# Attention probabilities turned through VectorE and DRAM instead of TensorE, in a two-block transformer kernel

## The reference

```
q = partial_rope(q)                    # 16 heads of 64
k = partial_rope(k)                    # 2 key heads, each shared by 8 query heads
s = q . k * 64**-0.5                   # chunks of 64 queries see their own and the two chunks before
m = max(max(s), sink)
p = exp(s - m)
o = (p / (sum(p) + exp(sink - m))) @ v # the probabilities are what is turned
a = (o * silu(za)) @ w_att_out
```

## Time and profile before

| | |
|---|---|
| median of three runs | 1270.37 us (1270.3 to 1270.75) |
| profiled execution | 1270.71 us, of it span 1268.9 |
| granted TensorE clock | 0.999 of full speed |
| TensorE busy | 1261.5 us, 99% |
| VectorE busy | 893.3 us, 70% |
| ScalarE busy | 619.7 us, 49% |
| GpSimd busy | 724.1 us, 57% |

### The profile page before, as it was taken

One profiled execution on the slowest core, in us unless ns is written; L12 is line 12 of the kernel. 1 busy time (PEld: TensorE's weight loads), 2 busy tenths in 40 slices (PEclk: granted clock), 3 DMA queues, 4 the chain that ended last, 5 costly groups with the idle time before them and its releaser, 6 DMA issues.

```text
span 1268.9 us, 19753 instructions
## 1 busy us (share of the span) xinstructions
PE 1261.5 (99%) x7542; PEld 1091.2 (86%) x7542; DVE 893.3 (70%) x1380; ACT 619.7 (49%) x989; POOL 724.1 (57%) x513
## 2 busy tenths in 40 slices
PE   9999999999999999999999999999999999999998
PEld 7877877777888899989988998877778899999886
DVE  6775555777444599558855869766656999998587
ACT  6123533565334555325522546354556656666454
POOL 3543433434543588658865866444333786666767
PEclk9999999999999999999999999999999999999999
DMA  7253176564423335353535335333522233225351
GB/s 225 87 150 108 42 199 159 144 187 125 124 75 100 100 100 166 100 166 100 167 101 166 103 106 174 108 88 88 137 67 68 76 121 100 89 83 199 100 210 73
DMA packets 205371, 154.89 MB, mean 122 GB/s; under 512 B 67488, under 2 KB 194976, under 8 KB 204512
## 3 DMA queue, kind: packets, MB, share of 16 engines
q1 hardware_dynamic: 204800, 153.06, 40.3%
q10 hardware_dynamic: 480, 0.59, 0.1%
HBM read 136.20 MB, written 14.16 MB: 118 GB/s over the span
## 4 chain that ended last, share of the span: by engine, by line
PE 96%; ACT 1%; DVE 1%; DMA 1%; POOL 1%; issue 0%; SPq 0%; ACTq 0%
PE gemm L961 16%; PE gemm L962 16%; PE gemm L969 16%; PE gemm L1235 10%; PE gemm L1234 10%; PE gemm L1239 10%; PE gemm L985 2%; PE gemm L986 2%; PE gemm L991 2%; PE gemm L1018 2%; PE gemm L1019 2%; PE gemm L1024 2%; PE mix L1355 1%; PE mix L1343 1%; PE mix L1332 1%; DMA raw<-w_in 1%
## 5 line engine op out<-in xcount | busy, mean ns | idle before, releaser
L793 POOL TENSOR_TENSOR wlo<-raw,whi 128x512 fp32r<-128x512 f32 x264 | 368.7, 1428 | 288.6 <-ACT whi L1491 269.1
L961 PE MATMUL gemm<-hh,whi 128*128 128x512 f32 x544 | 215.3, 396 | 0.2 <-ACT whi L1491 0.2
L962 PE MATMUL gemm<-hl,whi 128*128 128x512 f32 x544 | 212.4, 390 | 0.0
L813 POOL TENSOR_TENSOR wlo<-raw,whi 128x512 fp32r<-128x512 f32 x108 | 159.4, 1501 | 40.5 <-ACT whi L1685 32.4
L1491 ACT ACTIVATE whi<-raw 128x2048 fp32r<-128x2048 f32 x62 | 118.4, 1909 | 46.0 <-PE gemm L969 19.8
L969 PE MATMUL gemm<-hh,wlo 128*128 128x512 f32 x544 | 136.0, 391 | 0.0
L1234 PE MATMUL gemm<-hh,whi 128*128 128x256 f32 x496 | 124.8, 284 | 0.0
L961 PEld LDWEIGHTS gemm<-hh,whi 128*128 128x128 f32 x544 | 102.1, 188 | 26.3 <-issue 4.3
L1235 PE MATMUL gemm<-hl,whi 128*128 128x256 f32 x496 | 124.4, 284 | 0.0
L962 PEld LDWEIGHTS gemm<-hl,whi 128*128 128x128 f32 x544 | 102.3, 188 | 20.4
L969 PEld LDWEIGHTS gemm<-hh,wlo 128*128 128x128 f32 x544 | 101.7, 188 | 20.9
(11 more groups left out here) (545 smaller groups left out, 3124.6 us busy)
## 6 DMA issues: line engine op xcount, KB each, us to landing
raw<-w_in SPq DMA_DIRECT2D x53, 1024.0 KB, 5.3
raw<-w_gu SPq DMA_DIRECT2D x44, 512.0 KB, 5.2
raw<-w_down SPq DMA_DIRECT2D x16, 512.0 KB, 4.4
p_rows<-p_blocks SPq DMA_DIRECT2D x32, 160.0 KB, 3.2
p_t<-p_rows SPq DMA_DIRECT2D x8, 640.0 KB, 4.0
raw<-w_o SPq DMA_DIRECT2D x5, 1024.0 KB, 5.2
raw_b<-w_branch SPq DMA_DIRECT2D x16, 256.0 KB, 6.8
blk_b<-w_o SPq DMA_DIRECT2D x8, 512.0 KB, 7.1
```

Source lines behind the costliest of these rows:

```text
L793: last = nc.gpsimd.tensor_tensor(a(wlo), a(raw), as_f32(a(whi)), ALU.subtract)
L813: return nc.gpsimd.tensor_tensor(part_of(wlo, u, b), raw_block(u, f, k), as_f32(part_of(whi, u, b)), sub)
L961: mm(bank[:, :], w, xh[:, k, :], start=(k == 0), stop=False)
L962: mm(bank[:, :], w, xl[:, k, :], start=False, stop=False)
```

## The change

For the first 12 of the 16 v, the probabilities are no longer turned by TensorE. VectorE transposes them in blocks of 32x32 (`w_blockwise`) and sorts the blocks as it writes, into one of two buffers of 128x1024. SyncE stores the buffer with four DMAs of 128 KB (one for each 32 partitions) to `w_rows` in DRAM, in runs of 256 elements, waits until they have landed, and loads it back with one DMA of 512 KB into `w_turned_p`. TensorE multiplies with the values straight from there, reading four runs of 32 elements for each block of 128 queries, in slot 2v + 5. The last four v are handled as before. ScalarE's exponentials wait for the block transposes instead of TensorE's turns.

On SyncE's queue the stores and loads are placed by hand among the weight loads. The loads of the layer norm's scale, shift and the gate's bias (`lng`, `lnb`, `bsb`), whose memory the new buffers use, move from the end of the first block to behind the last values that read the buffers. In `turned_through` the wait for the output of two heads before is now ahead of the stores.

```diff
@@ constants, buffers
+        w_blocks = [place(f"w_blocks{i}", [P, 1024], Z0 + at) for i, at in enumerate((80, 98))]
+        w_turned_p = [place(f"w_turned_p{i}", [P, 1024], Z0 + 68 + 4 * i) for i in range(2)]
+        BY_DMA = 12
+        S_PE = 2 * BY_DMA
+        w_rows = nc.dram_tensor("w_rows", (2, P, 1024), f32, kind="Internal").ap()
@@ turned_through
                 sp.wait_ge(sem("p_turned"), i + 1)
-                for f in range(4):
...
                 if 2 <= i < HEADS + 2:
                     sp.wait_ge(sem("mo_o"), i - 1)
                 elif i >= HEADS + 2:
                     sp.wait_ge(sem("st_o"), i - HEADS - 1)
+                for f in range(4):
...
@@ SyncE
+            def store_probs(v):
+                sp.wait_ge(sem("w_tb"), v + 1)
+                if v >= 2:
+                    sp.wait_ge(sem("w_v"), 2 * v - 2)
+                for f in range(4):
+                    sp.dma_start(w_rows[v % 2].rearrange("(j a) c -> a j c", a=32)[:, :, 256 * f:256 * f + 256],
+                                 w_blocks[v % 2][32 * f:32 * f + 32, :].rearrange("a (j c) -> a j c", j=4)).then_inc(sem("w_stored"), 16)
+            def load_probs(v):
+                sp.wait_ge(sem("w_stored"), 64 * (v + 1))
+                sp.dma_start(w_turned_p[v % 2][:, :], w_rows[v % 2]).then_inc(sem("w_in"), 16)
...
+            load_wide(0)
+            store_probs(5)
+            load_probs(5)
+            store_probs(6)
+            load_probs(6)
             swap_rotary(3)
             store_turned(4)
+            load_wide(1)
+            store_probs(7)
+            store_turned(5)
+            load_probs(7)
+            load_wide(2)
+            store_probs(8)
+            store_turned(6)
+            load_probs(8)
+            load_wide(3)
+            store_turned(7)
+            for v in (9, 10):
+                store_probs(v)
+                load_probs(v)
+            slot_free(n_ao)
+            load(n_ao, cols(w_ao, 0, UC))
+            store_probs(11)
+            load_probs(11)
+            sp.wait_ge(sem("w_v"), S_PE)
+            sp.dma_start(lng[:, :], ln_g.partition_broadcast(P)).then_inc(sem("c2_in"), 16)
...
@@ TensorE, w_values
-                pe.wait_ge(sem("w_pt"), s + 1)
+                if s < S_PE:
+                    pe.wait_ge(sem("w_in"), 16 * (s // 2 + 1))
+                    by_block = w_turned_p[s // 2 % 2].rearrange("p (f k b) -> p k f b", k=8, b=32)
+                    turned = lambda k: by_block[:, s % 2 * 4 + k]
+                else:
+                    pe.wait_ge(sem("w_pt"), s - S_PE + 1)
+                    turned = lambda k: wpt[:, s % 2, k * P:(k + 1) * P]
@@ TensorE, w_slot
-                    for s in (i - 4, i - 3):
-                        if 0 <= s < STEPS:
-                            w_values(s)
-                if 0 <= i - 2 < STEPS:
+                first = i - 4 if i % 2 == 0 else i - 5
+                if (S_PE <= first < STEPS) if i % 2 == 0 else (0 <= first < S_PE):
+                    w_values(first)
+                    w_values(first + 1)
+                if S_PE <= i - 2 < STEPS:
                     w_turn(i - 2)
@@ ScalarE, w_exp
-                    if s >= 3:
-                        act.wait_ge(sem("w_t"), s - 2)
+                    if s >= S_PE + 3:
+                        act.wait_ge(sem("w_t"), s - 2 - S_PE)
+                    elif s >= 3:
+                        act.wait_ge(sem("w_tb"), (s - 3) // 2 + 1)
@@ VectorE
+            def w_blockwise(v_):
+                dve.wait_ge(sem("w_p"), 2 * v_ + 2)
+                if v_ >= 2:
+                    dve.wait_ge(sem("w_stored"), 64 * (v_ - 1))
+                blocks = w_blocks[v_ % 2].rearrange("p (j k b) -> p k j b", j=4, b=32)
+                for s in (2 * v_, 2 * v_ + 1):
+                    probs = wp[:, s % 3].rearrange("p h (k j b) -> p (h k) j b", j=4, b=32)
+                    own = blocks[:, s % 2 * 4:s % 2 * 4 + 4]
+                    if s % TT == 0:
+                        for k in (1, 3):
+                            last = v.transpose(own[:, k], probs[:, k])
+                    else:
+                        last = v.transpose(own, probs)
+                last.then_inc(sem("w_tb"), 1)
@@ VectorE, w_slot, behind w_norm(i // 2)
+                    if i < S_PE:
+                        w_blockwise(i // 2)
@@ VectorE, layer_norm_first
+                dve.wait_ge(sem("c2_in"), 64)
```

More of the change, by code:

```diff
@@ L630, in turned_through @@
                 sp.wait_ge(sem("p_turned"), i + 1)
-                for f in range(4):
-                    sp.dma_start(p_rows[i % 2].rearrange("(j a) (k c) -> a k j c", a=32, c=P)[:, :, :, 32 * f:32 * f + 32],
-                                 p_blocks[32 * f:32 * f + 32, :].rearrange("a (k j b) -> a k j b", j=4, b=32)).then_inc(sem("p_stored"), 16)
                 if 2 <= i < HEADS + 2:
@@ L637, in turned_through @@
                     sp.wait_ge(sem("st_o"), i - HEADS - 1)
+                for f in range(4):
+                    sp.dma_start(p_rows[i % 2].rearrange("(j a) (k c) -> a k j c", a=32, c=P)[:, :, :, 32 * f:32 * f + 32],
+                                 p_blocks[32 * f:32 * f + 32, :].rearrange("a (k j b) -> a k j b", j=4, b=32)).then_inc(sem("p_stored"), 16)
                 sp.wait_ge(sem("p_stored"), 64 * (i + 1))
@@ L719, in store_turned @@
                                  x_turned[m % 4][32 * f:32 * f + 32, :].rearrange("a (j b) -> a j b", b=32)).then_inc(sem("x_stored"), 16)
[L721 to L734, removed]
@@ L735, in _ @@
-            slot_free(n_vs)
+            def store_probs(v):
[8 more added lines that the diff above has]
+                sp.dma_start(w_turned_p[v % 2][:, :], w_rows[v % 2]).then_inc(sem("w_in"), 16)
@@ L736, in load_wide, with load_qz @@
+            def load_qz(n):
+                slot_free(n)
+                p, j = divmod(n - n_qz, 2)
+                load(n, cols(w_in2, (I2_ZA if j else I2_Q) + p * UC, UC))
             def load_wide(u):
+                slot_free(n_vs + u)
                 slot = raw[:, (n_vs + u) % 2].rearrange("p (k a) c -> p k (a c)", a=2)
                 load(n_vs + u, cols(w_in2, I2_VS + u // 2 * 512, 512, 4 * (u % 2), 4), slot)
+            load_qz(n_qz)
+            load_qz(n_qz + 1)
+            sp.wait_ge(sem("key_s"), 1)
@@ new lines, in _ @@
+            for a, b in ((0, 8), (8, 0)):
+                for kv in range(2):
+                    sp.dma_start(key_t[a:a + 8, kv, :], key_s[64 * kv + b:64 * kv + b + 8, :]).then_inc(sem("key_in"), 16)
+            load_qz(n_qz + 2)
+            swap_rotary(0)
+            load_qz(n_qz + 3)
+            load_qz(n_qz + 4)
+            store_probs(0)
+            swap_rotary(1)
+            load_probs(0)
+            store_turned(0)
+            load_qz(n_qz + 5)
+            store_probs(1)
+            store_turned(1)
@@ L740, in _ @@
+            load_probs(1)
+            load_qz(n_qz + 6)
+            store_probs(2)
+            load_probs(2)
+            store_probs(3)
+            load_probs(3)
+            swap_rotary(2)
+            store_turned(2)
+            load_qz(n_qz + 7)
+            store_probs(4)
+            store_turned(3)
+            load_probs(4)
             load_wide(0)
+            store_probs(5)
+            load_probs(5)
+            store_probs(6)
+            load_probs(6)
             swap_rotary(3)
@@ L743, in _ @@
+            sp.wait_ge(sem("w_v"), S_PE)
+            sp.dma_start(lng[:, :], ln_g.partition_broadcast(P)).then_inc(sem("c2_in"), 16)
+            sp.dma_start(lnb[:, :], ln_b.partition_broadcast(P)).then_inc(sem("c2_in"), 16)
+            sp.dma_start(bsb[:, :, :].rearrange("p g i -> p (g i)"), sg_b.partition_broadcast(P)).then_inc(sem("c2_in"), 16)
             for u in range(1, 4):
[L744 to L747, removed]
+                slot_free(n_ao + u)
+                load(n_ao + u, cols(w_ao, u * UC, UC))
@@ L1338, in w_turn @@
                 pe.wait_ge(sem("w_p"), s + 1)
-                if s >= 1:
-                    pe.wait_ge(sem("w_pt"), s)
+                if s > S_PE:
+                    pe.wait_ge(sem("w_pt"), s - S_PE)
                 for h in range(2):
@@ L1355, in w_values @@
                         last = mm(M[3][64 * h:64 * h + 64, c * P:(c + 1) * P], v2[:, c - 1 + kb_, kv * DH:(kv + 1) * DH],
-                                  wpt[:, s % 2, (2 * h + kb_) * P:(2 * h + kb_ + 1) * P],
+                                  turned(2 * h + kb_),
                                   start=(kb_ == keys_of(c)[0]), stop=(kb_ == 1))
@@ L1846, in w_turned @@
             def w_turned(s):
-                act.wait_ge(sem("w_t"), s + 1)
-                if s >= 2:
+                act.wait_ge(sem("w_t"), s + 1 - S_PE)
+                if s >= S_PE + 2:
                     act.wait_ge(sem("w_v"), s - 1)
@@ L2636, in _ @@
             T = tiles_before(n_e0)
-            dve.wait_ge(sem("c2_in"), 64)
+            dve.wait_ge(sem("c2_in"), 16)
             tile_ready(T)
```

(2 more changed lines are left out.)

4 lines of the change are left out of this document (removed).

## The result

The changed kernel takes 1273.93 us (median of seven executions, 1271.99 to 1275.72), the kernel before 1270.37 (seven, 1270.27 to 1270.75); the ratio is 1.0026, 95% interval 1.0015 to 1.0037. It is slower by 0.26%, where I had forecast 1264.2. The profiled execution took 1273.12, its span is 1271.3 at a granted clock of 0.999. The other six executions were granted 0.995 to 0.998, so the profile shows one of the milder ones.

The account below looks back on a forecast made before the run. TensorE, busy 1261.5 of 1268.9 us, was taken as the bound. Turns removed 7.1, less VectorE's 0.4 and the trip's 0.5, made 6.2 us, giving 1264.2; its own range was 1263 to 1266, the full range 1262.0 to 1268.3.

Parts of the forecast that it names:

- What goes from TensorE: Attention stage: turns of 24 of 32 steps leave, 8.0 us, less 0.5 and 0.4 for gaps: net 7.1 us.
- The moving operand: Values on TensorE: reading four runs of 32 elements instead of contiguous ones costs nothing extra.
- Rival 4: TensorE's 84 value products: reads in runs of 128 bytes make the kernel slower, 1275.5 if doubled; chance 0.06.
- VectorE, 0.4 us: 15 us of block transposes, mostly in idle time; lag of 1 to 1.5 us per v costs TensorE 0.4 us.
- The trip, 0.5 us: Through DRAM: 8.5 us (bounds 7.2 and 10.8) against five slots, with 0.5 us of waits in slots 23 to 27.
- SyncE's queue: Trip's stores, waits and loads stand among weight loads; the next weight load queues behind each wait, only one tightly.
- The tight load: Second wide unit's weight load, issued at 895.13 and split by ScalarE at 903.07, has 2.6 us to spare.
- The sum: 7.1 - 0.4 - 0.5 = 6.2 us gained, giving a median of 1264.2.
- Rival 2: VectorE's lag and the trip take 3 us or more, 1266 to 1269; chance 0.14.
- rival 3: Weight load held behind the stores stalls ScalarE by 6 us in sum, no gain, 1268 to 1272; chance 0.04.
- the trip's length: Slower by the DRAM trip itself: gain gone at 14.6 us, 1279 at a 17 us trip; chance 0.03.
- What would show it: Signs in the trace, such as TensorE's DMA waits on w_turned_p at v = 9 to 11 only, 1 us or less.

Follow-up runs that it names:

- run 9: The changed kernel with block transposes moved to the odd slot behind the gate product and the last four x2_rows stores behind the last probabilities load: 1265.26 us, 0.9962.
- run 4: The kernel before with the changed kernel's 30 block transposes added on VectorE at the same places, into an unread scratch buffer: 1274.97 us, 1.0030.
- run 12: The kernel before with the 30 block transposes added on VectorE in the odd slot, behind the multiplication for attention's output: 1270.34 us, 0.9999.
- run 10: The changed kernel with only the block transposes moved to the odd slot behind the gate product, SyncE's queue as it was: 1270.43 us, 0.9997.
- run 7: The changed kernel with only the last four x2_rows stores moved behind the last load of probabilities on SyncE's queue: 1275.01 us, 1.0036.
- run 1: The changed kernel with block transposes cut to one 128x32 per v (wrong probabilities), all transfers and waits kept: 1270.48 us, 0.9999.
- run 3: The changed kernel with short block transposes and also values from k2's columns that don't wait for the trip: 1264.40 us, 0.9955.
- run 2: The changed kernel with the first 24 steps' values computed from k2's columns, not waiting for the trip (wrong output), transposes and DMAs kept: 1274.38 us, 1.0031.

## Why the prediction was wrong

**What goes from TensorE, 7.1 us: the mechanism right, the term 1 us too large.** The six pairs came out at 1.02 each, 6.1 us; run 9's span is 1268.9 - 1262.8 = 6.1 below that of before (its profiled execution was the fastest of five; the medians differ by 5.2). The prediction named 6.2 as its bound with all gaps in full, and nearly so they came: in run 9 the large product ahead of the values at 849.40 starts 0.32 before them, and the one behind them takes 0.34 to its follower.

**The moving operand, 0: right.** 1.15 us after, 1.15 before. Rival 4 is out.

**VectorE, 0.4 us: this step failed.** The transposes' durations were right (670 and 291 ns in the median against the 0.67 to 0.70 taken). Wrong was to take their cost as a lag of 1 to 1.5 us a v in the wide stage, felt at softmax 12. I asked how busy VectorE is and not what stands behind the new work in its order. Behind it stands `att_t`, and behind that, through ScalarE's in-order copy, the weights of the large products. On the kernel before this alone costs 4.5 us (run 4), and nothing in the other place (run 12). The path from `att_t` to `wlo` had no term in the sum; it holds the longest wait, 2.10 us.

**The trip, 0.5 us: the length right in part, the start wrong.** From the store's issue to TensorE's start it is 10.0 us after, of which the load's issue is 6.2 in; in run 10 the trip takes 924.33 - 915.53 = 8.8. I had taken 8.5, bounds 7.2 and 10.8; v = 5, behind a fresh weight load, took 11.9, over the upper bound. The loads landed in 3.7 us in the median (taken: 3.6), the stores in 3.6, where I had said 2 to 3.2. What I left out above all is that the trip can't always start when its data are ready. With VectorE in good order a trip that starts late is enough to bring the kernel back to 1270.43 (run 10).

**SyncE's queue: this step failed too.** I followed what is queued behind the trip (the weight loads), and not what the trip is queued behind, though the diff shows `store_turned` ahead of the loads and stores of probabilities. In the change it holds the load for v = 4 back until VectorE has turned other rows, and in run 10 the store of v = 9 by 4.8 us. The tight load that I named was not what stalled: it went at 895.44 and ScalarE split it at 901.76, with 0.40 us of wait for it.

**The sum.** Forecast -7.1 + 0.9 = -6.2 us. Measured, in the stage: -6.1 + 8.8 = +2.7, of it 7.8 us in waits that the trace lists. Of the remaining 1 us I estimate 0.65 as part of the same waits: a wait is listed from the end of the product before it, which lasts 0.39, where without a wait scores or values would have started 0.32 behind that product's start and a large product 0.23 (seven waits and one). The last 0.3 stays open. The waits were some nine times what I put down, and the median execution of the change, at a granted clock of 0.998, is another 0.8 us longer; a fall of the clock had no term in the sum either. Rival 2 had the mechanism in part (a lag of VectorE and a late trip), with 1266 to 1269 at most; rival 3, a stall of ScalarE ahead of a weight split, has the other part, by another way than a late load. As slower kernels I had thought only of the operand and the trip's length; the operand cost nothing, and the trip's length is at most the wait of v = 5, 0.54 us.

**What would show it.** "Waits for a DMA on w_turned_p, at v = 9 to 11 only": they came at v = 4 and 5 too (0.58 and 0.54 us at 878.17 and 888.14), and the wait for `wlo` was on no list of mine.

## What to carry to other kernels

Work put on an engine with idle time was free here only where nothing that another engine waited for stood behind it (run 12 against run 4). So write down the order of the engine around the new work, and follow each result one engine further, here VectorE to ScalarE to GpSimd to TensorE. For a transfer, list what its queue holds ahead of it, with the time to issue, as well as behind. And where two causes each make the same thing late, undoing one can show nothing (run 7) or less than half of the gain (run 10); try both together before a cause is dropped.

## What the runs showed of the hardware

**TensorE's clock after a wait.** In run 10, TensorE's timeline around the longest wait, and the windows of all engines in the same stretch (PE, PEld, DVE, ACT and POOL busy, then the granted clock, DMA share, GB/s):

```profile
924.33 1.27 PE L1419 MATMUL mix<-w_turned_p,v 128*64 128x128 f32 x16 [3.49 <-DMA w_turned_p<-w_rows]
925.54 0.80 PE L1043 MATMUL gemm<-whi,hh 128*128 128x512 f32 x1
926.13 0.63 PE L1044 MATMUL gemm<-whi,hl 128*128 128x512 f32 x1
926.56 0.63 PE L1043 MATMUL gemm<-whi,hh 128*128 128x512 f32 x1
...
931.19 0.40 PE L1043 MATMUL gemm<-whi,hh 128*128 128x512 f32 x1
931.42 0.40 PE L1044 MATMUL gemm<-whi,hl 128*128 128x512 f32 x1
```

```profile
910.00:920.00 10.00, 9.45 (x61) 7.04 (x60) 7.67 (x19) 4.56 (x13) 4.20 (x3) 1.00 0.86 238
920.00:930.00 10.00, 6.51 (x36) 4.61 (x38) 4.41 (x12) 2.93 (x11) 2.04 (x2) 0.83 0.67 209
930.00:940.00 10.00, 10.00 (x77) 7.43 (x78) 5.93 (x14) 4.47 (x14) 3.97 (x4) 1.00 0.48 159
```

Behind a wait of 3.49 us the products start 0.43 us apart for a while, then 0.23 again: the lower level, 1.2 GHz, against 2.4. The granted clock of 0.83 over 10 us is 1.7 us lost on top of the wait. It explains the sum to within 0.1 us: run 10's span is 5.6 above run 9's, and it has 4.0 of waits and 1.7 of clock. In run 1, 5.8 us of waits cost 8.7 (1271.6 against run 3's 1262.9); in run 2, 6.3 cost 10.9. The runs with such waits also spread widely (run 10: 1267.06 to 1272.50, run 9: 1264.77 to 1266.33). In the changed kernel's profiled execution, whose longest wait is 2.1 us, the clock stayed at 1.00 in this stage. But the length of a wait doesn't decide it. In run 4 the clock fell behind a wait of 1.92 us (933.69):

```profile
930.00:940.00 10.00, 8.08 (x54) 6.28 (x53) 7.06 (x19) 3.20 (x12) 0.00 (x0) 0.83 0.29 99
```

And run 7 has the wait for `wlo` at the same place and of the same length as the change (2.08 and 2.10 us), and the clock fell only there: the scores that follow, first in run 7 and then in the change, take 1.56 and 0.88 us.

```profile
905.60 1.56 PE L1388 MATMUL mix<-k,q 64*64 64x192 f32 x16
904.78 0.88 PE L1390 MATMUL mix<-k,q 64*64 64x192 f32 x16
```

Behind run 7's longer wait, 2.77 us, it stayed at 1.00 (930 to 940). The Trainium skill, "TensorE: Matmul & The Clock Gate", HAM oscillation, says that a DMA wait of a few microseconds can put the array back to the slow level; the trace agrees for the waits of 2.9 to 3.5 us in runs 1 and 10, and shows a fall behind 1.9 and 2.1 us too. Such a wait can cost more than its length, by 1.7 us here, and from the wait alone one can't tell whether it will.

**VectorE beside GpSimd.** In the changed kernel (timeline of all engines), two multiply-adds of VectorE beside GpSimd:

```profile
922.12 6.35 POOL L851 TENSOR_TENSOR wlo<-raw,whi 128x512 fp32r<-128x512 f32 x4 [12.34 <-ACT whi L1556]
...
923.89 3.44 DVE L2814 SCALAR_TENSOR_TENSOR za_last<-za_e,za_last 128x512 f32<-128x512 f32 x2
```

The same line, with the same shapes, took 1.25 us at 893.62, with GpSimd idle. The scaling of four 128x128 took 3.94 us at 901.28 beside GpSimd, and 1.01 at 920.68 without it. Block transposes of `x_turned` beside GpSimd in run 9 (rows from its timeline) keep their time:

```profile
900.84 5.47 POOL L849 TENSOR_TENSOR wlo<-raw,whi 128x512 fp32r<-128x512 f32 x4 [2.08 <-ACT whi L1554]
...
902.60 1.29 DVE L2842 STREAM_TRANSPOSE x_turned<-prm_xT 128x512 f32<-128x512 f32 x2
```

1.29 us for two, 0.65 each. It can be GpSimd that loses: in run 9 the two multiply-adds at 860.50 take 1.29 us with GpSimd's unit starting at 860.41, and that unit takes 7.25 us instead of the 5.04 of the one before. The Trainium skill, "SBUF — State Buffer", SBUF: two separate sides, has VectorE and GpSimd exclude each other from a shared port pair where VectorE reads two operands from SBUF or runs in a two-port mode. The multiply-adds with two operands and the transposes with one agree with it; the scaling has one, and agrees only if it ran in such a mode, which no row tells. So in these traces an order on VectorE that moves such work into GpSimd's time costs more than the work's own duration; how much of the 4.5 us of run 4 that is, no run separates.
